# Falling column order in the dense products of a two-block network on one core

## The chip, the cores and the metric

The kernel runs on one core of a Trainium2 chip. The metric is the device time of one execution in microseconds (us). Three runs of the kernel before are at hand; one more execution was profiled.

## The reference

A sequence of 256 tokens with 1024 features goes through two small networks, one after the other. The parts that matter here are the dense products; everything between them (norms, rotary embedding, top-k attention, a recurrent scan, a convolution, a dilated attention) is left out:

```python
proj = h @ w_in                        # dsa: 1024 -> 2120 columns
y = o @ w_o                            # dsa_out: 1024 -> 1024
x = x + relu(h @ w_up) ** 2 @ w_down   # mlp0 and mlp1: 1024 -> 4096 -> 1024
r, k, v = mixed @ w_rkv                # rkv, then rwkv_out
... = h @ conv_w_in                    # conv: 1024 -> 4096, then conv_out
... = h @ dil_w_in                     # dil: 1024 -> 8192, then dil_out
```

All are float32. The kernel makes each product in three parts: a number is split into a rounded high part (`hi`, type fp32r) and the low rest (`lo`, fp32r), and hi x hi, hi x lo and lo x hi are added in PSUM.

## The kernel before

Weights come from HBM as granules of 128 x 1024 f32 into a ring of four slots (`raw`). ScalarE rounds a granule into `w_hi` (line 737), VectorE subtracts it to get `w_lo` (line 1350), and TensorE multiplies. Each of the three engines has one instruction order, written out by hand, and semaphores (`hi_ready`, `lo_ready`, `granule_used`) that count whole granules. So TensorE waits for a granule to be split, and the ring's slot comes free when its last matmul has ended.

Each matmul has a stationary operand (128 x 128, loaded by the weight load that goes with it), a moving operand (128 partitions x 256 or 512 columns) and an output tile of as many columns in one of the eight PSUM banks of 512 columns. The dense products come in two forms:

- by features (`feature_granule`, lines 2308 to 2310, and `entering_features`, line 2325): a 128-column piece of the weights is stationary, and the activation (`hi[:, kt, :]`, 256 tokens) moves. A granule holds two blocks of 128 input features by 512 output features and gives 24 matmuls of 256 columns.
- by tokens (`token_tile`, lines 2263 to 2265; `token_halves`, 2275 to 2277; `entering_tokens`, 2345; the value columns of the attention's input, 2536 to 2538; `down_tile` of the feed-forward, 2658 to 2660): 128 tokens of the activation are stationary, and 256 or 512 weight columns move.

The middle steps of the feed-forward and of the last projection are hardware loops (`pe.Fori`); the slots and banks in them are constants, and only the counts that are waited for depend on the loop's register.

The change leaves alone all other matmuls: plain f32 products (lines 2745, 2755, 2767), transposes (2375, 2401), the turns through a diagonal matrix (`turn_scaled`, line 2390), the broadcasts of the modulation (2724, 2730), the scan (2877 and others), the attention, the first granule of all (`opening_granule`) and the index columns. Two of these write PSUM columns in an order that isn't simply rising. In `turn_scaled` with `ordered=True` (the last turn, before the dilated attention's projection) the output is

```python
dst = bank[banks[b]][:, kk * SEQ:(kk + 1) * SEQ].rearrange("p (i f a l) -> p f a i l", i=TILES, f=TILES, a=32)[:, i]
```

with l of size 2 and i of stride 128: pairs of neighbouring columns, with a jump of 128 columns between them. `turn_heads` (line 2375) writes pairs with a stride of 4 columns.

Of the kernel before, what the change touches and what calls it, by code (L numbers as in the profile page):

```python
# [14 lines left out]
P = 128  # L15
# [11 lines left out]
BLOCK = 512  # L27
PER_BLOCK = 4
RING = 4
# [125 lines left out]
def program(nc, A, out):  # L155
    parts, parts_bf = shape_constants()
    with ExitStack() as keep:
# [29 lines left out]
        w_hi = sb("w_hi", [P, RING, GRAN], F32R)  # L187
        w_lo = sb("w_lo", [P, RING, GRAN], F32R)
# [16 lines left out]
        view, at = {}, 0  # L205
# [4 lines left out]
        at = 0  # L210
# [1134 lines left out]
        def _(dve):  # L1345
# [906 lines left out]
            conv()  # L2252
            dilated()

        @block.tensor
        def _(pe):
            def token_tile(i, slot, hi, lo, kts, n, dst, first, last):

                for kk, kt in enumerate(kts):
                    at = slice(kk * n, (kk + 1) * n)  # L2260
                    x_hi, x_lo = hi[:, kt, i * P:(i + 1) * P], lo[:, kt, i * P:(i + 1) * P]
                    begin, end = first and kk == 0, last and kk == len(kts) - 1
                    pe.matmul(dst, x_hi, w_hi[:, slot, at], start=begin, stop=False, skip_group_check=True)  # L2263
                    pe.matmul(dst, x_hi, w_lo[:, slot, at], start=False, stop=False, skip_group_check=True)  # L2264
                    mm = pe.matmul(dst, x_lo, w_hi[:, slot, at], start=False, stop=end, skip_group_check=True)  # L2265
                return mm

            def token_halves(i, slot, hi, lo, q, dst, parts=range(4)):

                for part in parts:  # L2270
                    kk, h = part // 2, part % 2
                    cols = slice(kk * BLOCK + h * SEQ, kk * BLOCK + (h + 1) * SEQ)
                    x_hi, x_lo = (x[:, 2 * q + kk, i * P:(i + 1) * P] for x in (hi, lo))
                    to = dst[:, h * SEQ:(h + 1) * SEQ]
                    pe.matmul(to, x_hi, w_hi[:, slot, cols], start=q == part == 0, stop=False, skip_group_check=True)  # L2275
                    pe.matmul(to, x_hi, w_lo[:, slot, cols], start=False, stop=False, skip_group_check=True)  # L2276
                    mm = pe.matmul(to, x_lo, w_hi[:, slot, cols], start=False, stop=q == PER_BLOCK - 1 and kk == 1, skip_group_check=True)  # L2277
                return mm

            def halves_granule(g, hi, lo, q, banks, begun=0):  # L2280
# [37 lines left out]
            def entering_features(g, slot, hi, lo, q, banks, rounded, split, change=False):  # L2318

                def term(w, x, begin, end):  # L2320
                    for f in range(4):
                        dst = banks[f // 2][:, (f % 2) * SEQ:(f % 2 + 1) * SEQ]
                        for kk in range(2):
                            at = slice(kk * BLOCK + f * P, kk * BLOCK + (f + 1) * P)
                            mm = pe.matmul(dst, w[:, slot, at], x[:, 2 * q + kk, :], start=begin and kk == 0 and f % 2 == 0,  # L2325
                                           stop=end and kk == 1, skip_group_check=True)
# [12 lines left out]
            def entering_tokens(gs, hi, lo, qs, banks, tiles, rounded, split):  # L2339

                def term(x, w, begin, end):
                    for i in tiles:
                        for g, q in zip(gs, qs):
                            for kk in range(2):
                                mm = pe.matmul(banks[i], x[:, 2 * q + kk, i * P:(i + 1) * P], w[:, g % RING, kk * BLOCK:(kk + 1) * BLOCK],  # L2345
                                               start=begin and q == kk == 0, stop=end and q == PER_BLOCK - 1 and kk == 1, skip_group_check=True)
# [99 lines left out]
            def dsa():  # L2446
                base = STREAM["dsa"]
                hi, lo = act_hi[0], act_lo[0]
# [75 lines left out]
                for q in range(PER_BLOCK):  # L2524
                    g = base + 4 + q
                    slot = g % RING
                    pe.wait_ge(lo_ready, g + 1)
                    feature_granule(g, slot, hi, lo, q, (bank[2],), range(2), False)
                    for i in range(TILES):
                        for kk in range(2):  # L2530
                            kt = 2 * q + kk
                            at = slice(kk * BLOCK + KV_COLS, (kk + 1) * BLOCK)
                            x_hi, x_lo = hi[:, kt, i * P:(i + 1) * P], lo[:, kt, i * P:(i + 1) * P]
                            dst = bank[3][:, i * KV_COLS:(i + 1) * KV_COLS]
                            begin, end = q == 0 and kk == 0 and i == 0, q == PER_BLOCK - 1 and kk == 1
                            pe.matmul(dst, x_hi, w_hi[:, slot, at], start=begin, stop=False, skip_group_check=True)
                            pe.matmul(dst, x_hi, w_lo[:, slot, at], start=False, stop=False, skip_group_check=True)
                            mm = pe.matmul(dst, x_lo, w_hi[:, slot, at], start=False, stop=end, skip_group_check=True)
# [101 lines left out]
            def mlp(l):  # L2640
                base, done = STREAM[f"mlp{l}"], 2 * FF_STEPS * l
                hi, lo = act_hi[0], act_lo[0]
# [8 lines left out]
                def down_tile(i, n, q, at_slot, slot, first, last):  # L2651

                    x_hi, x_lo = (m[:, slot, q, i * P:(i + 1) * P] for m in (M["hi"], M["lo"]))
                    wide = SEQ
                    for h in range(BLOCK // wide):
                        at = slice(n * BLOCK + h * wide, n * BLOCK + (h + 1) * wide)
                        dst = bank[2 + 2 * i + n][:, h * wide:(h + 1) * wide]
                        pe.matmul(dst, x_hi, w_hi[:, at_slot, at], start=first and q == 0 and h == 0, stop=False, skip_group_check=True)  # L2658
                        pe.matmul(dst, x_hi, w_lo[:, at_slot, at], start=False, stop=False, skip_group_check=True)  # L2659
                        mm = pe.matmul(dst, x_lo, w_hi[:, at_slot, at], start=False, stop=last and q == PER_BLOCK - 1, skip_group_check=True)  # L2660
                    return mm

                def wait_down(it, k0, q):
# [575 lines left out]
```

## Time and profile before

| | |
|---|---|
| median of 3 runs | 1062.45 us (1061.2 to 1068.3) |
| span of the profiled execution | 1066.7 us |
| TensorE matmuls busy | 1048.1 us (98%), 10480 matmuls |
| VectorE busy | 771.7 us (72%) |
| ScalarE busy | 590.3 us (55%) |
| GpSimd busy | 120.4 us (11%) |
| DMA | 192.23 MB, mean 180 GB/s |

The span is the time from the first to the last instruction of one profiled execution; no separate run time is given for that execution. Its span is 4.3 us above the median of the three runs and lies between the lowest and the highest of them. Matmuls are pipelined, and the duration of one reaches into the next, so busy time says that the engine has work and not how fast it goes; the pace comes from how many start in a stretch.

### The profile page before, as it was taken

Reading aid. Unit: us, or ns where it says so; the run is one execution under the profiler, and the core shown is the slowest. Engines: PE = TensorE matmul, PEld = TensorE weight load, DVE = VectorE, ACT = ScalarE, POOL = GpSimd, SP = SyncE. Lnnn points to the kernel's source line nnn. Section 1 sums busy time; section 2 is a strip of 40 time slices with the busy share of each in tenths; the row PEclk is TensorE's granted clock in tenths of the full one; section 3 lists DMA queues with packets and bytes.
Section 4 is the critical chain, followed back from the end, with each engine's and each line's share of the span. In section 5 each row is a group of like instructions: output and inputs, shape, how many; then the busy total and the mean of one; then the engine's idle time right before and its main releaser. Section 6 shows DMA issues by size and latency. Waiting matters only on the chain.

```text
span 1066.7 us, 25458 instructions
## 1 busy us (share of the span) xinstructions
PE 1048.1 (98%) x10480; PEld 996.2 (93%) x10485; DVE 771.7 (72%) x1090; ACT 590.3 (55%) x900; POOL 120.4 (11%) x131
## 2 busy tenths in 40 slices
PE   9999999999999999999999999999999999999997
PEld 8966999999999899997899999999998999999985
DVE  5987666766789689768766676786676877775586
ACT  6586555555456783334555454564544667666452
POOL 0230010100000028841000000000000000000000
PEclk9999999999999999999999999999999999999999
DMA  8734687888634510002678777737653656556401
GB/s 308 251 90 137 216 286 266 271 296 280 204 122 155 163 61 5 3 11 74 217 250 287 255 252 264 276 121 228 197 192 112 212 181 199 171 195 196 143 2 59
DMA packets 83073, 192.23 MB, mean 180 GB/s; under 512 B 6000, under 2 KB 6912, under 8 KB 82992
## 3 DMA queue, kind: packets, MB, share of 16 engines
q1 hardware_dynamic: 74256, 159.93, 45.3%
q0 software_dynamic: 7584, 27.53, 7.8%
q10 hardware_dynamic: 1152, 3.59, 1.0%
q8 instruction: 63, 1.03, 0.4%
q14 instruction: 18, 0.15, 0.0%
HBM read 189.45 MB, written 1.05 MB: 179 GB/s over the span
## 4 chain that ended last, share of the span: by engine, by line
PE 88%; DVE 6%; issue 2%; ACT 2%; DMA 2%; POOL 0%; DVEq 0%; POOLq 0%; ACTq 0%
PE bank L2308 13%; PE bank L2310 13%; PE bank L2309 13%; PE bank L2659 5%; PE bank L2658 5%; PE bank L2660 5%; PE bank L2325 4%; PE bank L2345 4%; PE bank L2877 4%; PE bank L2275 2%; PE bank L2276 2%; PE bank L2277 2%; PE bank L2263 1%; PE bank L2265 1%; PE bank L2264 1%
## 5 line engine op out<-in xcount | busy, mean ns | idle before, releaser
L1350 DVE TENSOR_TENSOR w_lo<-raw,w_hi 128x1024 fp32r<-128x1024 f32 x295 | 357.8, 1223 | 199.2 <-ACT w_hi L737 198.7
L737 ACT ACTIVATE w_hi<-raw 128x1024 fp32r<-128x1024 f32 x295 | 310.3, 1059 | 291.4 <-PE bank L2310 150.4
L2308 PE MATMUL bank<-act_hi,w_hi 128*128 128x256 f32 x1200 | 334.0, 278 | 0.4 <-DVE w_lo L1350 0.3
L2309 PE MATMUL bank<-act_lo,w_hi 128*128 128x256 f32 x1200 | 332.9, 277 | 0.0
L2310 PE MATMUL bank<-act_hi,w_lo 128*128 128x256 f32 x1200 | 332.8, 277 | 0.0
L2308 PEld LDWEIGHTS bank<-act_hi,w_hi 128*128 128x128 f32 x1200 | 225.3, 188 | 1.7 <-DVE w_lo L1350 0.9
L2310 PEld LDWEIGHTS bank<-act_hi,w_lo 128*128 128x128 f32 x1200 | 225.3, 188 | 0.0
L2309 PEld LDWEIGHTS bank<-act_lo,w_hi 128*128 128x128 f32 x1200 | 225.0, 187 | 0.0
L2658 PE MATMUL bank<-w_hi,ff_hi 128*128 128x256 f32 x512 | 141.5, 276 | 0.0
L2659 PE MATMUL bank<-w_lo,ff_hi 128*128 128x256 f32 x512 | 141.5, 276 | 0.0
L2660 PE MATMUL bank<-w_hi,ff_lo 128*128 128x256 f32 x512 | 141.5, 276 | 0.0
L2658 PEld LDWEIGHTS bank<-w_hi,ff_hi 128*128 128x128 f32 x512 | 96.1, 188 | 0.0
L2660 PEld LDWEIGHTS bank<-w_hi,ff_lo 128*128 128x128 f32 x512 | 96.1, 188 | 0.0
L2659 PEld LDWEIGHTS bank<-w_lo,ff_hi 128*128 128x128 f32 x512 | 96.1, 188 | 0.0
L590 POOL DMA_DIRECT2D mod_w<-in_w_mod_dram x48 | 25.8, 538 | 319.2 <-DVE mod_all L1666 239.2
L2275 PE MATMUL bank<-w_hi,act_hi 128*128 128x256 f32 x192 | 54.2, 282 | 0.0
L2276 PE MATMUL bank<-w_lo,act_hi 128*128 128x256 f32 x192 | 53.8, 280 | 0.0
L2277 PE MATMUL bank<-w_hi,act_lo 128*128 128x256 f32 x192 | 53.8, 280 | 0.0
L1666 DVE SCALAR_TENSOR_TENSOR mod_all<-mod_w,c_col,mod_all 128x1024 f32<-128x1024 f32 x42 | 52.5, 1278 | 0.0
L561 POOL TENSOR_TENSOR stat<-stat,half_neg 128x1 f32<-128x1 f32 x10 | 5.5, 553 | 405.9 <-DVE stat L1364 372.6
L2275 PEld LDWEIGHTS bank<-w_hi,act_hi 128*128 128x128 f32 x192 | 36.7, 191 | 1.0 <-issue 1.0
L2276 PEld LDWEIGHTS bank<-w_lo,act_hi 128*128 128x128 f32 x192 | 36.0, 188 | 0.0
(375 smaller groups left out, 1675.4 us busy)
## 6 DMA issues: line engine op xcount, KB each, us to landing
raw<-in_mlp_w_up_dram SPq DMA_DIRECT2D x64, 512.0 KB, 3.7
raw<-in_mlp_w_down_dram SPq DMA_DIRECT2D x64, 512.0 KB, 6.1
raw<-in_dil_w_in_dram SPq DMA_DIRECT2D x64, 512.0 KB, 4.1
mod_w<-in_w_mod_dram POOLq DMA_DIRECT2D x48, 512.0 KB, 5.9
raw<-in_conv_w_in_dram SPq DMA_DIRECT2D x32, 512.0 KB, 4.5
raw<-in_rwkv_w_rkv_dram SPq DMA_DIRECT2D x24, 512.0 KB, 4.1
raw<-in_dsa_w_in_dram SPq DMA_DIRECT2D x12, 512.0 KB, 8.1
raw<-in_dsa_w_o_dram SPq DMA_DIRECT2D x8, 512.0 KB, 4.5
```

The source lines that it names most:

```text
L737: act.activation(w_hi[:, slot, :], raw[:, slot, :], ACT.Copy).then_inc(hi_ready, 1)
L1350: dve.tensor_tensor(w_lo[:, slot, :], raw[:, slot, :], w_hi[:, slot, :].bitcast(F32), ALU.subtract).then_inc(lo_ready, 1)
L1666: dve.scalar_tensor_tensor(total, part, c, total, ALU.mult, ALU.add).then_inc(mod_used[n], 1)
L2275: pe.matmul(to, x_hi, w_hi[:, slot, cols], start=q == part == 0, stop=False, skip_group_check=True)
L2276: pe.matmul(to, x_hi, w_lo[:, slot, cols], start=False, stop=False, skip_group_check=True)
L2277: mm = pe.matmul(to, x_lo, w_hi[:, slot, cols], start=False, stop=q == PER_BLOCK - 1 and kk == 1, skip_group_check=True)
L2308: pe.matmul(dst, w_hi[:, slot, at], hi[:, kt, :], start=begin, stop=False, skip_group_check=True)
L2309: pe.matmul(dst, w_hi[:, slot, at], lo[:, kt, :], start=False, stop=False, skip_group_check=True)
L2310: mm = pe.matmul(dst, w_lo[:, slot, at], hi[:, kt, :], start=False, stop=end, skip_group_check=True)
L2658: pe.matmul(dst, x_hi, w_hi[:, at_slot, at], start=first and q == 0 and h == 0, stop=False, skip_group_check=True)
L2659: pe.matmul(dst, x_hi, w_lo[:, at_slot, at], start=False, stop=False, skip_group_check=True)
L2660: mm = pe.matmul(dst, x_lo, w_hi[:, at_slot, at], start=False, stop=last and q == PER_BLOCK - 1, skip_group_check=True)
```

## The change

A helper takes an operand, moves its start address to the last column and negates the step of the last dimension. It is put around the moving operand and the output of every dense product in the two forms above. The stationary operand, the order of matmuls, the waits and the flags stay.

```diff
+        def falling(x):
+            x = x[:, :]
+            steps = [list(pair) for pair in x.ap]
+            first = x.offset + steps[-1][0] * (steps[-1][1] - 1)
+            return bass.AP(x.tensor, first, steps[:-1] + [[-steps[-1][0], steps[-1][1]]])
...
-                        pe.matmul(dst, w_hi[:, slot, at], hi[:, kt, :], start=begin, stop=False, skip_group_check=True)
-                        pe.matmul(dst, w_hi[:, slot, at], lo[:, kt, :], start=False, stop=False, skip_group_check=True)
-                        mm = pe.matmul(dst, w_lo[:, slot, at], hi[:, kt, :], start=False, stop=end, skip_group_check=True)
+                        pe.matmul(falling(dst), w_hi[:, slot, at], falling(hi[:, kt, :]), start=begin, stop=False, skip_group_check=True)
+                        pe.matmul(falling(dst), w_hi[:, slot, at], falling(lo[:, kt, :]), start=False, stop=False, skip_group_check=True)
+                        mm = pe.matmul(falling(dst), w_lo[:, slot, at], falling(hi[:, kt, :]), start=False, stop=end, skip_group_check=True)
```

The same is done in `token_tile`, `token_halves`, `entering_features`, `entering_tokens`, the value columns and `down_tile`.

## Rows read from the trace of the kernel before

**Rows 1.** The page: span, busy time of three engines, TensorE's granted clock in 40 slices.

```profile
span 1066.7 us, 25458 instructions
...
PE 1048.1 (98%) x10480; PEld 996.2 (93%) x10485; DVE 771.7 (72%) x1090; ACT 590.3 (55%) x900; POOL 120.4 (11%) x131
...
PEclk9999999999999999999999999999999999999999
```

**Rows 2.** The page: the chain that ended last, by engine.

```profile
PE 88%; DVE 6%; issue 2%; ACT 2%; DMA 2%; POOL 0%; DVEq 0%; POOLq 0%; ACTq 0%
```

**Rows 3.** Groups of TensorE by shape: count, busy us, mean ns of one.

```profile
L2308 PE MATMUL bank<-act_hi,w_hi 128*128 128x256 f32 x1200 | 334.0, 278 | 0.4 <-DVE w_lo L1350 0.3
...
L2658 PE MATMUL bank<-w_hi,ff_hi 128*128 128x256 f32 x512 | 141.5, 276 | 0.0
...
L2275 PE MATMUL bank<-w_hi,act_hi 128*128 128x256 f32 x192 | 54.2, 282 | 0.0
...
L2263 PE MATMUL bank<-w_hi,act_hi 128*128 128x512 f32 x72 | 28.7, 399 | 0.0
...
L2325 PE MATMUL bank<-act_hi,w_hi 128*128 128x256 f32 x184 | 25.6, 281 | 0.6 <-ACT act_hi L768 0.6
...
L2345 PE MATMUL bank<-w_hi,act_hi 128*128 128x512 f32 x56 | 15.8, 404 | 0.1
...
L2536 PE MATMUL bank<-w_hi,act_hi 128*128 128x256 f32 x16 | 4.5, 279 | 0.0
```

**Rows 4.** Windows of TensorE alone: stretch, its length, busy us (matmuls), clock, DMA share, GB/s.

```profile
180.00:290.00 110.00, 110.00 (x970) 1.00 0.80 270
...
830.00:950.00 120.00, 120.00 (x1021) 1.00 0.60 193
```

**Rows 5.** Timeline of TensorE near 100 us: start, length, instruction, count (512 columns).

```profile
99.62 1.10 PE L2345 MATMUL bank<-w_lo,act_hi 128*128 128x512 f32 x4
100.55 1.10 PE L2345 MATMUL bank<-w_hi,act_lo 128*128 128x512 f32 x4
```

**Rows 6.** Timeline of TensorE near 352 us: plain f32 operands, 256 columns.

```profile
352.01 7.07 PE L2755 MATMUL bank<-act_f,g 128*80 128x256 f32 x32
359.01 1.07 PE L2813 MATMUL bank<-bk,const 128*32 128x256 f32 x16
```

**Rows 7.** Timeline of TensorE at three turns (ordered, plain, by heads) and their followers.

```profile
816.67 1.95 PE L2390 MATMUL bank<-per_head,X 128*128 128x128 f32 x16
818.45 1.88 PE L2730 MATMUL bank<-mod_all,const 128*128 128x512 f32 x4
820.29 2.05 PE L2390 MATMUL bank<-per_head,X 128*128 128x128 f32 x16
...
701.79 3.82 PE L2390 MATMUL bank<-per_head,xn 128*128 128x128 f32 x32
705.45 1.84 PE L2724 MATMUL bank<-const,mod_all 128*128 128x1 f32 x16
...
1038.66 0.60 PE L2375 MATMUL bank<-const,z_dil 128*128 128x128 f32 x4
1039.01 1.18 PE L2345 MATMUL bank<-w_hi,act_hi 128*128 128x512 f32 x4
```

**Rows 8.** TensorE's wait on a granule's low part, and VectorE's group that makes it.

```profile
PE bank L2308 <- DVE w_lo L1350: 0.3, 1, 0.3
...
L1350 DVE TENSOR_TENSOR w_lo<-raw,w_hi 128x1024 fp32r<-128x1024 f32 x295 | 357.8, 1223 | 199.2 <-ACT w_hi L737 198.7
```

More of the change, by code:

```diff
@@ L2262, in token_tile @@
                     begin, end = first and kk == 0, last and kk == len(kts) - 1
-                    pe.matmul(dst, x_hi, w_hi[:, slot, at], start=begin, stop=False, skip_group_check=True)
-                    pe.matmul(dst, x_hi, w_lo[:, slot, at], start=False, stop=False, skip_group_check=True)
-                    mm = pe.matmul(dst, x_lo, w_hi[:, slot, at], start=False, stop=end, skip_group_check=True)
+                    pe.matmul(falling(dst), x_hi, falling(w_hi[:, slot, at]), start=begin, stop=False, skip_group_check=True)
+                    pe.matmul(falling(dst), x_hi, falling(w_lo[:, slot, at]), start=False, stop=False, skip_group_check=True)
+                    mm = pe.matmul(falling(dst), x_lo, falling(w_hi[:, slot, at]), start=False, stop=end, skip_group_check=True)
                 return mm
@@ L2274, in token_halves @@
                     to = dst[:, h * SEQ:(h + 1) * SEQ]
-                    pe.matmul(to, x_hi, w_hi[:, slot, cols], start=q == part == 0, stop=False, skip_group_check=True)
-                    pe.matmul(to, x_hi, w_lo[:, slot, cols], start=False, stop=False, skip_group_check=True)
-                    mm = pe.matmul(to, x_lo, w_hi[:, slot, cols], start=False, stop=q == PER_BLOCK - 1 and kk == 1, skip_group_check=True)
+                    pe.matmul(falling(to), x_hi, falling(w_hi[:, slot, cols]), start=q == part == 0, stop=False, skip_group_check=True)
+                    pe.matmul(falling(to), x_hi, falling(w_lo[:, slot, cols]), start=False, stop=False, skip_group_check=True)
+                    mm = pe.matmul(falling(to), x_lo, falling(w_hi[:, slot, cols]), start=False, stop=q == PER_BLOCK - 1 and kk == 1, skip_group_check=True)
                 return mm
@@ L2324, in term @@
                             at = slice(kk * BLOCK + f * P, kk * BLOCK + (f + 1) * P)
-                            mm = pe.matmul(dst, w[:, slot, at], x[:, 2 * q + kk, :], start=begin and kk == 0 and f % 2 == 0,
+                            mm = pe.matmul(falling(dst), w[:, slot, at], falling(x[:, 2 * q + kk, :]), start=begin and kk == 0 and f % 2 == 0,
                                            stop=end and kk == 1, skip_group_check=True)
@@ L2344, in term @@
                             for kk in range(2):
-                                mm = pe.matmul(banks[i], x[:, 2 * q + kk, i * P:(i + 1) * P], w[:, g % RING, kk * BLOCK:(kk + 1) * BLOCK],
+                                mm = pe.matmul(falling(banks[i]), x[:, 2 * q + kk, i * P:(i + 1) * P], falling(w[:, g % RING, kk * BLOCK:(kk + 1) * BLOCK]),
                                                start=begin and q == kk == 0, stop=end and q == PER_BLOCK - 1 and kk == 1, skip_group_check=True)
@@ L2535, in dsa @@
                             begin, end = q == 0 and kk == 0 and i == 0, q == PER_BLOCK - 1 and kk == 1
-                            pe.matmul(dst, x_hi, w_hi[:, slot, at], start=begin, stop=False, skip_group_check=True)
-                            pe.matmul(dst, x_hi, w_lo[:, slot, at], start=False, stop=False, skip_group_check=True)
-                            mm = pe.matmul(dst, x_lo, w_hi[:, slot, at], start=False, stop=end, skip_group_check=True)
+                            pe.matmul(falling(dst), x_hi, falling(w_hi[:, slot, at]), start=begin, stop=False, skip_group_check=True)
+                            pe.matmul(falling(dst), x_hi, falling(w_lo[:, slot, at]), start=False, stop=False, skip_group_check=True)
+                            mm = pe.matmul(falling(dst), x_lo, falling(w_hi[:, slot, at]), start=False, stop=end, skip_group_check=True)
                     mm.then_inc(granule_used, 1)
@@ L2657, in down_tile @@
                         dst = bank[2 + 2 * i + n][:, h * wide:(h + 1) * wide]
-                        pe.matmul(dst, x_hi, w_hi[:, at_slot, at], start=first and q == 0 and h == 0, stop=False, skip_group_check=True)
-                        pe.matmul(dst, x_hi, w_lo[:, at_slot, at], start=False, stop=False, skip_group_check=True)
-                        mm = pe.matmul(dst, x_lo, w_hi[:, at_slot, at], start=False, stop=last and q == PER_BLOCK - 1, skip_group_check=True)
+                        pe.matmul(falling(dst), x_hi, falling(w_hi[:, at_slot, at]), start=first and q == 0 and h == 0, stop=False, skip_group_check=True)
+                        pe.matmul(falling(dst), x_hi, falling(w_lo[:, at_slot, at]), start=False, stop=False, skip_group_check=True)
+                        mm = pe.matmul(falling(dst), x_lo, falling(w_hi[:, at_slot, at]), start=False, stop=last and q == PER_BLOCK - 1, skip_group_check=True)
                     return mm
```

## The prediction

> **What bounds the kernel now.** I read the page's first two parts, then the chain that ended last, then the groups of TensorE by shape, then windows and stretches of its timeline, because the change touches nothing but the operands of matmuls. The reader is to see first that TensorE is busy 1048.1 of 1066.7 us and idle for 18.6, that VectorE and ScalarE have 295 and 476 us of free time, and that TensorE's granted clock is 9 tenths or more in all 40 slices, so this is one single stretch at the upper of its two levels, 2.4 GHz [rows 1]. The chain agrees: 88% of it is TensorE [rows 2]. Whatever the change does to the time from one matmul to the next therefore comes out in the end nearly in full. A few per cent of the matmuls' records can be missing, so I take paces only from stretches whose counts are plausible.
>
> The "mean ns of one" of a matmul is no pace. A matmul of 256 columns shows 276 to 282 ns [rows 3], yet 970 of them start in 110 us [rows 4]: they overlap, and the pace is 110 / 970 = 113.4 ns. That is the number that counts. Another dense stretch, 830 to 950 us, has 1021 in 120 us, or 117.5 ns [rows 4]. I take 115 ns for the whole kernel. With 512 columns four matmuls take 100.55 - 99.62 = 0.93 us, or 233 ns each [rows 5]. At 2.4 GHz one column takes 0.417 ns, so 256 columns are 106.7 ns and 512 are 213.3: the changed matmuls run within 6 to 10% of one column a tick, and no wait stands between them.
>
> **The change part by part.** Counted from the groups, the changed matmuls of 256 columns are 3 x 1200 + 3 x 512 + 3 x 192 + 3 x 184 + 3 x 16 = 6312, and those of 512 columns 3 x 72 + 3 x 56 = 384 [rows 3] (each line of rows 3 stands for three of the same count, one for each product of a high and a low part). They hold 6312 x 0.115 + 384 x 0.233 = 726 + 89 = 815 us of TensorE's time. The other 250 us (the scan, the attention, transposes, the last norm and the output) keep their operands as they are.
>
> Removed and added: no instruction, no wait, no semaphore increment, no DMA. The helper runs when the program is built and gives each matmul another start address and a step of -1 instead of 1. All the slots and banks are constants there, also inside the loops, so no register arithmetic is added to TensorE's queue; cost nothing, and there is no cover that could go. The order of matmuls, the weight loads, the flags and the columns that each writes stay. Both operands fall, so column c of the moving tile still goes to column c of PSUM, and two products that add to one tile still touch each column exactly one whole matmul apart. The readers of the banks wait for the whole group as before. Where VectorE fills w_lo (1223 ns a granule) it signals after the whole granule, so that no reader can start early or late because of the direction [rows 8].
>
> What is left is the price of a column that is read in falling order from SBUF and of one that is written in falling order to PSUM. No row of the trace shows a step of -1 on either side, so I bound it.
>
> From below: the column's own tick. If the 6.7 to 20 ns by which a matmul exceeds its columns were owed to the rising order, falling could give back at most 6312 x (115 - 106.7) + 384 x (233 - 213.3) = 52 + 8 = 60 us, which would be 1062 - 60 = 1002 us. Nothing in the trace ties that excess to the order, and I take none of it.
>
> From above: the nearest rows at half the column rate are the products whose operands are plain f32. There, 32 matmuls of 256 columns take 359.01 - 352.01 = 7.00 us, or 219 ns each [rows 6], and four of 512 columns take 820.29 - 818.45 = 1.84 us, or 460 ns each [rows 7]. If each column in falling order were taken by itself where two are taken together now, the changed matmuls would go at that pace: 6312 x (219 - 115) + 384 x (460 - 233) = 656 + 87 = 743 us more.
>
> Nearest to the change are the writes whose order isn't simply rising. The turn at 816.67 us (line 2390, ordered) writes 128 columns as pairs, each pair 128 columns from the one before, and 16 of them take 818.45 - 816.67 = 1.78 us, 111 ns each [rows 7]. The same operation with plain rising columns takes (705.45 - 701.79) / 32 = 114 ns [rows 7]. The transposes at 1038.66 us write pairs 4 columns apart, four in 0.35 us [rows 7]. So the PSUM side doesn't need a rising run of columns, and a jump after each pair is free. These rows keep the order inside a pair, and falling turns exactly that round. They also spend twice as long on a column as the changed products, so they could hide a loss that the change would show. I take zero because a falling pair still lies in the same two neighbouring words as the rising one, and the rows with jumps show that neighbourhood within a pair and not the direction of travel is what the writes are served by; both ends stay for the range.
>
> The Trainium skill speaks against this. Its page "PSUM — Partial Sum Buffer", section "Specifications (TRN2)", says that PSUM has lines of 8 bytes and that any non-contiguous access pattern slows matmuls significantly; "Advanced Engine Details and Errata", section "PSUM Cachelines", asks that every two consecutive elements be contiguous. By the first wording the turn at 816.67 us should be slow, and it isn't; by the second it may be fast, and a falling pair is an open case. For the moving tile, "SBUF Cachelines" on the same page asks for two accesses in a row to one line of 16 bytes; falling columns make four, as rising ones do, and by that rule the reads cost nothing more.
>
> **The rivals.** (a) *No change.* The address pattern is followed at the same pace in either direction: 1062 us. For it: the rows with jumps, and the lack of any added instruction. Against it: no row with a negative step. That the change does not do what it says (the pattern reaches the engine as a rising one) would give the same time, and is counted here, with 3 of the 54 in 100.
>
> (b) *Half rate.* The slower end, one mechanism: in a product at one column a tick, two neighbouring columns are served in one access, and the pair is only recognised when the second lies above the first. Its place is the PSUM write or the moving read of 6696 matmuls; its price is 743 us by the rows above. It decides from the first matmul on, since TensorE has no slack there. Of the 18.6 us of idle time [rows 1], a wait such as the 0.3 us of line 2308 for w_lo [rows 8] would vanish in it, as the weights would be ready long before; I take 15 us off. 1062 + 743 - 15 = 1790 us. If the pace were exactly two ticks a column (213.3 and 427 ns) the sum would be 6312 x 98.3 + 384 x 194 - 15 = 680 us and the time 1742. For it: the changed products are the ones that run close to one column a tick, the only ones that need pairs served together. Against it: nothing but the rows with jumps. It is also what the rule on PSUM's lines gives in this kernel, in the strict reading of the Trainium skill's page "PSUM — Partial Sum Buffer".
>
> (c) *A small price a matmul.* A falling tile starts on an odd column (255 or 511), and a lost tick or a short refill there costs a few ns a matmul. From 1.6 ns on (10.6 / 6696) it is over 1%. The pace of the same matmuls already differs by 117.5 - 113.4 = 4.1 ns between two stretches [rows 4]; by that much it would be 6696 x 4.1 = 27 us, 1090 us.
>
> (d) *Faster.* The excess of 6.7 to 20 ns shrinks, since reads of the moving tile and the weight load meet in another order: at most 1002 us, and half of it 1032.
>
> **How the numbers follow.** A measurement of this kernel can tell about 1%, 10.6 us, from no change; the three runs shown span 1061.2 to 1068.3. The profiled execution spans 1066.7 us, 4.3 above the median of 1062.45 and inside those three, so I add the sums to 1062. Chances: (a) 0.54, (b) 0.36, (c) 0.06, (d) 0.04. The likeliest is (a), 1062 us, and its own range is 1054 to 1072. Leaving (b) out would leave more than 2 in 10 out, so the range reaches over it: up to 1810, the 1790 with the spread of the paces. The low end is that of (a), since (d) has 4 in 100. Faster by over 1%: (d), 0.04. Slower by over 1%: (b) and most of (c), 0.41. Within 1%: the rest, 0.55.
>
> **What would show it.** In the changed kernel's windows the dense stretch from 180 to 290 us should again hold about 970 matmuls, the groups of line 2308 should stay near 278 ns, and four of 512 columns should take 0.93 us. Under (b) that stretch would hold about 500, with VectorE's and ScalarE's shares of the span falling by 40% and TensorE's staying at 98%. Under (c) all three would be off by a few ns. The unchanged stretches (the scan from 399 to 486 us, line 2390) should keep their lengths in every case; if they don't, the cause isn't the direction. My prediction is wrong above all if the order within a pair matters, which no row here tests.

## The result

The changed kernel takes 1092.88 us (median of 4 runs, 1092.71 to 1093.33) against 1061.83 us before: a ratio of 1.0267, with a 95% interval of 1.0224 to 1.0310. It is slower by 31 us, where no change was forecast.

The page of the changed kernel, its span, busy times and chain:

```profile
span 1091.2 us, 25458 instructions
...
PE 1073.8 (98%) x10480; PEld 1022.0 (94%) x10485; DVE 772.2 (71%) x1090; ACT 590.3 (54%) x900; POOL 119.9 (11%) x131
...
PEclk9999999999999999999999999999999999999999
...
PE 90%; DVE 5%; issue 1%; DMA 1%; ACT 1%; DVEq 0%; POOLq 0%; POOL 0%; ACTq 0%
...
L2314 PE MATMUL bank<-act_hi,w_hi 128*128 128x256 f32 x1200 | 339.1, 283 | 0.0
```

The instruction count and the granted clock are those of [rows 1]; VectorE and ScalarE are as busy in us as before. TensorE has 25.7 us more and the span 24.5. The mean of one matmul in the largest group went from 278 [rows 3] to 283 ns, which looks like nothing much; the pace is what to read. A window of TensorE in the changed kernel, the columns as in [rows 4]:

```profile
180.00:290.00 110.00, 110.00 (x927) 1.00 0.78 264
```

In that stretch 927 matmuls stand where 970 stood [rows 4]: 118.7 ns each, not 113.4. And its timeline for the kinds that were costed apart (512 columns; plain f32):

```profile
99.94 1.09 PE L2351 MATMUL bank<-w_hi,act_hi 128*128 128x512 f32 x4
100.87 1.10 PE L2351 MATMUL bank<-w_lo,act_hi 128*128 128x512 f32 x4
...
361.06 7.07 PE L2761 MATMUL bank<-act_f,g 128*80 128x256 f32 x32
368.06 1.07 PE L2819 MATMUL bank<-bk,const 128*32 128x256 f32 x16
```

Four falling matmuls of 512 columns take 0.93 us, as in [rows 5]. The plain f32 products keep their 7.00 us [rows 6], and the ordered turn takes 840.31 - 838.53 = 1.78 us in the changed kernel too [rows 7]. So the loss is all in the 6312 matmuls of 256 columns.

Their starts fall on a few levels. Before, a feature product starts 113.3 or 117.8 ns after the one ahead of it, for tens of us on end. It is 113.3 throughout the convolution and in both feed-forwards behind their first 20 us, and 117.8 in those 20 us, in the second block's first products and in the dilated attention's. After, the feature products are at 120.0 ns and the token products at 117.8. By stages, from the start of each one's first product, the first feed-forward lost 7.2 us, the second 7.3, the convolution 5.1, the dilated attention 2.6, the second block 1.0 and the first attention 0.8, with 0.4 before it: 24.4 of the 24.5.

The other 6.5 us of the 31 are in the kernel before. Its runs on one chip fall into two groups: of the 13 beside the first experiments, nine took 1060.5 to 1063.7 us and four 1067.5 to 1068.7. The profiled one, 1066.7 us, is of the second: its dilated attention ran at 117.8. A later kernel with the same paces elsewhere (halves, below) spans 1059.7 us and has that stretch at 113.3. The 1536 products of that stage at 4.4 ns each would be 6.8 of the 7.0 us between the two spans (an estimate). The changed kernel has no such spread (0.6 us).

### The profile page after: what moved, and what is told of

It is laid out like the page before. It is cut to its first block, busy times and chain, and to the rows that moved or that the text cites. A ratio compares the mean times of both kernels' runs of the same rounds, so it can differ in the third digit from the quotient of the medians.

```text
span 1091.2 us, 25458 instructions
## 1 busy us (share of the span) xinstructions
PE 1073.8 (98%) x10480; PEld 1022.0 (94%) x10485; DVE 772.2 (71%) x1090; ACT 590.3 (54%) x900; POOL 119.9 (11%) x131
## 4 chain that ended last, share of the span: by engine, by line
PE 90%; DVE 5%; issue 1%; DMA 1%; ACT 1%; DVEq 0%; POOLq 0%; POOL 0%; ACTq 0%
PE bank L2314 13%; PE bank L2316 13%; PE bank L2315 13%; PE bank L2666 6%; PE bank L2665 6%; PE bank L2664 6%; PE bank L2331 5%; PE bank L2351 4%; PE bank L2883 3%; PE bank L2281 2%; PE bank L2283 2%; PE bank L2282 2%; PE bank L2269 1%; PE bank L2271 1%; PE bank L2270 1%
## 5 line engine op out<-in xcount | busy, mean ns | idle before, releaser
L2314 PE MATMUL bank<-act_hi,w_hi 128*128 128x256 f32 x1200 | 339.1, 283 | 0.0
L2316 PE MATMUL bank<-act_hi,w_lo 128*128 128x256 f32 x1200 | 338.5, 282 | 0.0
L2315 PE MATMUL bank<-act_lo,w_hi 128*128 128x256 f32 x1200 | 338.5, 282 | 0.0
L2666 PE MATMUL bank<-w_hi,ff_lo 128*128 128x256 f32 x512 | 144.5, 282 | 0.0
L2665 PE MATMUL bank<-w_lo,ff_hi 128*128 128x256 f32 x512 | 144.4, 282 | 0.0
L2283 PEld LDWEIGHTS bank<-w_hi,act_lo 128*128 128x128 f32 x192 | 36.1, 188 | 0.0
```

Source lines behind the costliest of these rows:

```text
L2283: mm = pe.matmul(falling(to), x_lo, falling(w_hi[:, slot, cols]), start=False, stop=q == PER_BLOCK - 1 and kk == 1, skip_group_check=True)
L2314: pe.matmul(falling(dst), w_hi[:, slot, at], falling(hi[:, kt, :]), start=begin, stop=False, skip_group_check=True)
L2315: pe.matmul(falling(dst), w_hi[:, slot, at], falling(lo[:, kt, :]), start=False, stop=False, skip_group_check=True)
L2316: mm = pe.matmul(falling(dst), w_lo[:, slot, at], falling(hi[:, kt, :]), start=False, stop=end, skip_group_check=True)
L2665: pe.matmul(falling(dst), x_hi, falling(w_lo[:, at_slot, at]), start=False, stop=False, skip_group_check=True)
L2666: mm = pe.matmul(falling(dst), x_lo, falling(w_hi[:, at_slot, at]), start=False, stop=last and q == PER_BLOCK - 1, skip_group_check=True)
```

## The experiments

All whole-network times are compared with runs of the kernel before on the same chip. "Feature form" and "token form" are those of the section on the kernel, here "feature products" and "token products". The letters and numbers of the theories are explained in the expectation where each first appears.

**Which side.** The two sides of a matmul apart; the tiles come out reversed, so what follows computes with reversed tiles.

```diff
-pe.matmul(falling(dst), w_hi[:, slot, at], falling(hi[:, kt, :]), ...)
+pe.matmul(falling(dst), w_hi[:, slot, at], hi[:, kt, :], ...)     # e1, in all dense products
+pe.matmul(dst, w_hi[:, slot, at], falling(hi[:, kt, :]), ...)     # e2, in all dense products
```

> Only the PSUM side of every dense product falls; the moving tile is read rising, so each output tile comes out with its columns in reverse order and what follows computes with reversed tiles. Theory W (a falling write costs a few ns a matmul): all of the loss stays, about 1093 us, with the feature products near 120 ns apart. Theory R (a falling read costs it): about 1062 us, paces of 113.4 and 117.7 ns as before. Theory P (the pace depends on how the moving reads stand to the weight loads, and falling reads never get into the fast one): as R.

> Only the moving tile is read in falling order; PSUM is written rising, so the tiles again come out reversed. Theory W: about 1062 us. Theories R and P: about 1093 us, feature products near 120 ns and token products near 117.8 ns. If both sides had a price of their own, this and the run before would each lose a part, together 31 us.

Measured: writes alone 1063.21 us (ratio 1.0002, 0.9972 to 1.0032); reads alone 1092.84 us (1.0274, 1.0229 to 1.0318). The same stretch in each, first with falling writes:

```profile
180.00:290.00 110.00, 110.00 (x970) 1.00 0.80 269
```

and with falling reads:

```profile
180.00:290.00 110.00, 110.00 (x927) 1.00 0.78 262
```

970 is the kernel before and 927 the changed one, to the matmul. Falling writes cost nothing that these runs can tell; the whole loss is the moving read. Theory W has fallen.

**Which form.** Both sides fall in one form only.

```diff
-outF, inF, outT, inT = falling, falling, falling, falling
+outF, inF, outT, inT = falling, falling, rising, rising     # e3: feature form alone
+outF, inF, outT, inT = rising, rising, falling, falling     # e4: token form alone
```

> Both sides fall in the feature form alone (4152 matmuls of 256 columns); the token form rises as before. From the paces of the changed kernel (feature products 115.6 to 120.2 ns, that is 4.6 ns each on 4152) all theories give about 19 us if the two forms are independent: 1081 us. If token products are fast only because the matmuls before them left the engine in its fast pace, they lose their 4.2 ns too and the time is 1088 to 1093 us.

> Both sides fall in the token form alone (2160 matmuls of 256 columns, 384 of 512). Independent forms: 1536 products of the feed-forward lose 4.2 ns each, about 7 us, 1069 us. If the fast pace of 113.4 ns is entered only by rising token products (in the kernel before it begins at the first product of line 2658, at 140.5 us, and holds through the feature products that follow), the feature products lose it as well: 2 x 768 in the feed-forward, some 500 in the first attention, at 4.3 ns each, 9 us more: about 1078 us.

Measured: 1091.46 us (1.0260) and 1078.67 us (1.0140, 1.0095 to 1.0184). Each alone they lose 29 and 16 us, and both at once 31, not 45: they are not independent. Each form slows the other. In e3 the token products rise, and in the feed-forwards they go at 117.8 ns, where they had 113.3 before. In e4 no feature product is touched, and yet the convolution's (740 to 790 us) go at 117.8 ns: 427 in 50 us, where the kernel before has 444:

```profile
740.00:790.00 50.00, 50.00 (x427) 1.00 0.62 190
880.00:940.00 60.00, 60.00 (x532) 1.00 0.63 202
```

The second row is the other way round: the dilated attention (880 to 940 us) is at 113.3 here, with 532 matmuls, and was at 117.8 with 512 in the profiled run of the kernel before. So rising feature products have two paces, and what else ran in the kernel changes which of them a stage gets. That can't be a price of a matmul's own falling order. The expectation's 1078 us was met, but not its mechanism, by which the fast pace is entered only through rising token products: the dilated attention has the fast pace here although the token products of all dense stages fall. (One product of `change_form`, which the change leaves alone, still rises, at 313 us; the feature products are at 117.8 ns on both sides of it.)

**What of the order.** Three other orders, on both sides of all dense products; each leaves the result as it is.

```diff
-return bass.AP(x.tensor, first, steps[:-1] + [[-steps[-1][0], steps[-1][1]]])
+return bass.AP(x.tensor, x.offset + 1, steps[:-1] + [[2, n // 2], [-1, 2]])            # e5: 1, 0, 3, 2, ...
+return bass.AP(x.tensor, x.offset + n - 2, steps[:-1] + [[-2, n // 2], [1, 2]])        # e6: 254, 255, 252, 253, ...
+return bass.AP(x.tensor, x.offset + n // 2, steps[:-1] + [[-(n // 2), 2], [1, n // 2]]) # e7: 128 to 255, 0 to 127
```

> Both sides of all dense products go up, but inside each pair the upper column comes first (1, 0, 3, 2, ...). If the order within a pair is what costs, 1093 us; if the direction of travel or the place where the read starts costs, 1060 to 1066 us.

> Both sides go down by pairs, and inside a pair rise (254, 255, 252, 253, ...). If the direction of travel costs, about 1093 us; if only the order within a pair does, 1060 to 1066 us.

> Each tile is read and written upper half first, rising within each half (128 to 255, then 0 to 127; for 512 columns 256 to 511 first). If only the start or the end of a moving read against the next weight load counts, and not its direction, the pace changes here as well (towards 1093 us or otherwise away from 1062); if each column's step counts, 1060 to 1066 us.

Measured: swapped pairs 1063.11 us (1.0018, 0.9984 to 1.0052), falling pairs 1092.71 us (1.0275, 1.0217 to 1.0333), halves 1061.91 us (1.0001, 0.9976 to 1.0026). Falling by pairs costs what falling by columns costs, to 0.2 us, though it starts on an even column and rises inside each pair. Swapped pairs start on an odd column and cost nothing. What costs is the direction of travel through the tile, not the order in a pair, the start column or the jump at a half. The halves kernel runs as fast as the faster group of the kernel before, and its trace shows how these runs probably look (none of them was profiled):

```profile
740.00:790.00 50.00, 50.00 (x443) 1.00 0.62 192
880.00:940.00 60.00, 60.00 (x532) 1.00 0.59 188
```

Both stretches are at 113.3, and its span is 1059.7 us.

**The products by themselves.** A kernel of nothing but matmuls, in parts of 96 on a line each; features with `w` stationary and `act` moving, tokens the other way. VectorE, ScalarE and the queues are idle and there is no wait.

```python
features(lambda d, s, m: pe.matmul(d, s, m, **K))                                    # line 119, 121, ...
features(lambda d, s, m: pe.matmul(order(d, "fall"), s, order(m, "fall"), **K))      # line 120
```

> Not the network: 26 parts of 96 matmuls (the 512-column ones 48), one after another on the same SBUF data, each on a line of its own, with no other engine at work and no waits between them. The output holds a few PSUM banks and nothing of the reference. Theory 1 (the pace comes from the engine's own two read streams): the levels 113.4, 117.8 and 120.0 ns of the network's kernels appear here too, with all other engines idle: falling features 120.0, falling reads with rising writes 120.0, falling writes with rising reads 113.4 or 117.8, falling token products 117.8. Theory 2 (it is contention with VectorE's and ScalarE's traffic in SBUF): all parts run at one pace, below 113.4 ns. For the other orders: if the order inside a pair of columns counts, the swapped pairs are slow and falling pairs and fours are fast; if the direction of travel counts, the reverse. 512 columns: no difference above 1 ns. Plain f32 operands and bf16 operands: within 1 ns by order if the loss belongs to the pairing with a weight load of fp32r.

Its timeline: start, length, line, operands, count. The pace of a part is the way to the next part's start over its count.

```profile
62.66 11.68 PE L119 MATMUL bank<-act,w 128*128 128x256 f32 x96
74.17 11.53 PE L120 MATMUL bank<-act,w 128*128 128x256 f32 x96
85.54 11.67 PE L121 MATMUL bank<-act,w 128*128 128x256 f32 x96
...
131.44 11.68 PE L125 MATMUL bank<-act,w 128*128 128x256 f32 x96
142.96 11.53 PE L126 MATMUL bank<-act,w 128*128 128x256 f32 x96
154.33 11.67 PE L127 MATMUL bank<-w,act 128*128 128x256 f32 x96
...
246.14 11.07 PE L135 MATMUL bank<-w,act 128*128 128x512 f32 x48
257.05 11.37 PE L136 MATMUL bank<-w,act 128*128 128x512 f32 x48
268.25 41.60 PE L137 MATMUL bank<-af,wf 128*128 128x256 f32 x192
```

Rising (119) takes 11.51 us, 119.9 ns each, and falling (120) 11.37 us, 118.4: here falling is the *faster* one. Falling writes alone (125) 120.0, falling reads alone (126) 118.4: again the read. Swapped pairs and halves (128, 134) gave 120.0, falling pairs and fours 118.4. Theory 2 is out, since the parts run at two paces with all other engines idle, and neither is below 113.4 ns. But the sign is the opposite of the network's, which none of my theories gave. With 512 columns the sign is the network's own: rising (135) 227.3 ns, falling (136) 233.3. Plain f32 (137, 192 records for 96 matmuls) takes 41.4 us both ways, and bf16 (139, 140) 109.2 ns between neighbouring starts, both ways. Beside the idle engines, two things differed from the network: the moving tiles start at the weights' place in a block of 512 bytes, and nothing adds up in PSUM.

**Places in SBUF.** The same parts with the moving tile shifted by `d` columns:

```python
flat[:, kt * 256 + d:kt * 256 + d + 256]     # d = 0 to 144; 144 columns (576 bytes) is the network's
```

> Not the network: parts of 96 matmuls each on a line of its own (512 columns: 48), no other engine at work, four bf16 matmuls between most parts; the output is nothing of the reference. In the part-by-part run before, the moving tiles began 0 bytes from the weights' place in a block of 512 bytes; in the network they begin 64 bytes beyond it (576 of 1024). Here the start of the moving tile is shifted by 0 to 64 columns (0 to 256 bytes) and by 144 columns (576 bytes, as in the network), rising and falling. Theory A (two read streams of TensorE, moving tile and weight load, get in each other's way by their places in SBUF): the pace depends on the shift; at 144 columns rising gives 113.4 or 117.8 ns and falling 120.0, at 0 rising 120.0 and falling 118.4 as before. Theory B (it is the adding up in PSUM): the parts with 144 columns that only write stay at 120.0 and 118.4, those that add go to 113.4 or 117.8 and 120.0. Theory C (the other engines' traffic, or the network's waits, set the pace): all parts at 120.0 and 118.4 ns. For the form of the product: a feature part straight after a rising token part runs at 113.4 and after a falling token part at 117.8 if the fast pace is entered through token products alone.

The parts at 144 columns (149 and 151 write, 153 and 155 add up; then tokens and the features behind them, rising in 161, falling in 164):

```profile
205.73 11.76 PE L151 MATMUL bank<-act,w 128*128 128x256 f32 x96
217.34 0.61 PE L115 MATMUL bank<-ab,wb 128*128 128x256 bf16 x4
217.70 11.55 PE L153 MATMUL bank<-act,w 128*128 128x256 f32 x96
229.09 0.61 PE L115 MATMUL bank<-ab,wb 128*128 128x256 bf16 x4
...
243.17 11.14 PE L161 MATMUL bank<-w,act 128*128 128x256 f32 x96
254.15 11.04 PE L162 MATMUL bank<-act,w 128*128 128x256 f32 x96
265.03 0.61 PE L115 MATMUL bank<-ab,wb 128*128 128x256 bf16 x4
265.40 11.55 PE L164 MATMUL bank<-w,act 128*128 128x256 f32 x96
276.79 11.47 PE L165 MATMUL bank<-act,w 128*128 128x256 f32 x96
288.10 0.61 PE L115 MATMUL bank<-ab,wb 128*128 128x256 bf16 x4
```

At the network's place falling features take 11.61 us (120.9 with the start behind bf16) and rising ones 11.39 (118.6): the network's sign. Writing and adding give the same, so theory B is out. Features straight behind rising tokens take 10.88 us, 113.3 ns, and behind falling tokens 11.31, 117.8: the network's levels, to 0.1 ns. With no shift they were 120.0 and 118.4. With 512 columns at the network's place (lines 167 and 169) 48 matmuls take 11.29 us in either direction, so the 6 ns of the first bench are gone as well. Theory A stands in this bench. The next run asks what leads into the fast pace.

> Not the network: groups of 48 feature products (shift of 144 columns, as in the network), a few token products, 48 feature products again; four bf16 matmuls ahead of each group; other engines idle, the output is nothing of the reference. Theory M (two steady paces for rising order, 117.8 and 113.4 ns; a rising token product or a few switch to the fast one, which then holds; falling order leaves it and never enters it): the first feature part of each group runs at 117.8, the one behind n rising token products at 113.4 from some n between 1 and 4 on, behind falling token products at 117.8; a falling feature part behind 12 rising token products runs at 120.0, and the rising feature part behind that at 117.8 again; four bf16 matmuls end the fast pace. Theory N (the pace is set by which operands are read, and what came before does not count): every rising feature part has the same pace.

Groups of feature products, a few rising token products, features again. Here with one token product (125), with six (141), and a falling feature part (158) that came behind twelve, with a rising one (159) after it:

```profile
33.27 0.28 PE L125 MATMUL bank<-w,act 128*128 128x256 f32 x1
33.39 5.82 PE L126 MATMUL bank<-act,w 128*128 128x256 f32 x48
39.05 0.61 PE L119 MATMUL bank<-ab,wb 128*128 128x256 bf16 x4
...
81.07 0.86 PE L141 MATMUL bank<-w,act 128*128 128x256 f32 x6
81.76 5.60 PE L142 MATMUL bank<-act,w 128*128 128x256 f32 x48
87.20 0.61 PE L119 MATMUL bank<-ab,wb 128*128 128x256 bf16 x4
...
131.40 5.92 PE L158 MATMUL bank<-act,w 128*128 128x256 f32 x48
137.16 5.81 PE L159 MATMUL bank<-act,w 128*128 128x256 f32 x48
142.81 0.61 PE L119 MATMUL bank<-ab,wb 128*128 128x256 bf16 x4
```

Behind one or two token products the features stay at 117.9 ns; behind three, four, six or twelve they are at 113.3 to 113.5. Falling features are at 120.0 behind twelve token products, and the rising ones behind those at 117.7. That is theory M, with one flaw: three groups came out of the bf16 matmuls in the fast pace already (115.0 to 115.2 ns with the start), and in the one of them that had twelve rising token products and then rising features, these were at 117.7. One rising token product of 512 columns behind the third such group did the same (117.9). A token run can switch in either direction.

**Switching in the network.** Three rising token products ahead of four feature stages, in the kernel before and in the changed one. The stretch that the expectation calls the convolution's (830 to 950 us) is in truth the dilated attention's.

```diff
+            def into_pace(b, x, g):
+                pe.wait_ge(lo_ready, g + 1)
+                for k in range(3):
+                    pe.matmul(bank[b][:, 0:SEQ], x[:, k % 2, 0:P], w_hi[:, g % RING, 0:SEQ], start=True, stop=True)
```

> The kernel before, rising order, with three token products of 256 columns put ahead of four feature stages (two of the values, keys and rates of the second block, the second of the convolution's input, the second of the dilated attention's); each writes a bank half that the next product overwrites. Theory M (rising order has two steady paces, and three token products switch from the slow one to the fast one): some 288 + 672 + 1056 products go from 117.8 to 113.4 ns, 9 us, less 12 x 0.12 = 1.4 us for the added ones: 1053 to 1055 us, with the convolution's stretch (830 to 950 us) at 113.4. If a switch only toggles, and the waits in the network spoil it, the time lies between 1055 and 1068 us. Theory N (no such switch in the network): 1063 us.

> The same twelve added products (rising themselves) in the changed kernel, all dense products falling. Theory M: falling feature products have one pace, 120.0 ns, that nothing switches: 1092.9 + 1.4 = 1094 us. Theory N or any theory in which falling order only fails to find the way into the fast pace: 9 to 13 us faster than the changed kernel, about 1082 us.

Measured: 1073.19 us (1.0099, 1.0084 to 1.0115) and 1093.44 us (1.0299, 1.0285 to 1.0313). The first is a miss: not 9 us faster but 11 slower. Its windows say why:

```profile
740.00:790.00 50.00, 50.00 (x427) 1.00 0.62 190
880.00:940.00 60.00, 60.00 (x512) 1.00 0.56 178
```

The convolution was in the fast pace (444 matmuls in the kernel before) and is out of it (427); so is the dilated attention, which the halves kernel has at 113.3. The timeline just ahead of the added products (L2322) tells the two apart, first the convolution, then the dilated attention:

```profile
718.25 1.07 PE L2331 MATMUL bank<-act_hi,w_lo 128*128 128x256 f32 x8
719.16 0.52 PE L2322 MATMUL bank<-w_hi,act_hi 128*128 128x256 f32 x3
...
837.76 1.10 PE L2331 MATMUL bank<-act_hi,w_lo 128*128 128x256 f32 x8
838.70 0.52 PE L2322 MATMUL bank<-w_hi,act_hi 128*128 128x256 f32 x3
```

In the convolution the eight products ahead of the added three take 0.91 us, 114 ns each: there three token products led out of the fast pace. In the dilated attention they take 0.94 us, 118 ns each: it was slow from its first products on, and stayed slow. The two places in the second block were at 117.8 ns ahead of the added products and behind them. So at none of the four places did three token products lead into the fast pace, as they did in the bench, and why the dilated attention began slow in this kernel isn't shown. The sizes fit: added matmuls 1.4 us, 672 products of the convolution at 4.4 ns each 3.0, and the 1536 of the dilated attention 6.8, against a run that has it fast, make 11.2 of the 11.3 us.

The falling kernel gained nothing either (0.6 us slower than 1092.88). Theory M expected that, but it tells little, since the added products gained nothing in the rising kernel.

**The decisive pair.** One tensor of 64 bytes a partition is allocated ahead of the weights' ring, not behind it; weights and activations then start at the same place in a block of 512 bytes, as in the first bench.

```diff
+        gain = sb("gain", [P, 2, KT])
         raw = sb("raw", [P, RING, GRAN])
...
-        gain = sb("gain", [P, 2, KT])
```

> Not the network: for each of 14 places of the moving tile (shifted by 0 to 124 columns of 4 bytes against the weights' place in a block of 512 bytes) 12 token products, 48 feature products, 3 token products, 48 feature products, all rising, then 48 feature products falling; other engines idle, the output is nothing of the reference. Theory A (places and direction together set the pace): rising parts at 120.0 for 0 columns, at 113.4 or 117.8 for 16 (the network's place), falling at 118.4 for 0 and 120.0 for 16; other places have paces of their own, and one may keep both rising parts at 113.4 or below. Theory D (falling order is slow as such): falling is above rising at every place.

> The kernel before with one small tensor (64 bytes a partition) allocated ahead of the weights' ring and not behind it, so that the weights and the activation tiles start at the same place in a block of 512 bytes, not 64 bytes apart. Nothing else changes. Theory A: rising products of 256 columns go at 120.0 ns as in the first part-by-part run, 6312 x about 5 ns = 31 us more, less 384 x 6 ns for the wide ones: about 1090 us. Theory D: 1062 us.

> The changed kernel with the same move. Theory A: falling products at 118.4 ns: about 6312 x 1.2 = 8 us less than the changed kernel's 1092.9, so 1085 us, and below the moved rising kernel. Theory D: 1093 us, 31 us above the moved rising kernel.

Measured: rising 1094.95 us (1.0296, 1.0266 to 1.0327), falling 1086.95 us (1.0221, 1.0191 to 1.0251). With the weights moved by 64 bytes, falling order is the faster by 8.0 us, where before it was the slower by 31; the ranges of their runs (1094.26 to 1095.56, 1086.63 to 1087.19) lie far apart. Both are slower than the kernel before, and 5 and 2 us above what was expected. The rising kernel, moved:

```profile
180.00:290.00 110.00, 110.00 (x919) 1.00 0.78 258
```

and the falling one, moved:

```profile
180.00:290.00 110.00, 110.00 (x932) 1.00 0.78 261
```

919 against 932: 119.7 against 118.0 ns. With 512 columns the moved kernels go the other way: about 227 ns rising and 233 falling, as in the first bench. In the bench of places, at no shift and at 16 columns (the network's 64 bytes), features rising (125, 127; 149, 151) and falling (128; 152):

```profile
35.19 5.92 PE L127 MATMUL bank<-act,w 128*128 128x256 f32 x48
40.95 5.84 PE L128 MATMUL bank<-act,w 128*128 128x256 f32 x48
46.64 0.61 PE L119 MATMUL bank<-ab,wb 128*128 128x256 bf16 x4
...
106.23 5.61 PE L149 MATMUL bank<-act,w 128*128 128x256 f32 x48
111.67 0.52 PE L150 MATMUL bank<-w,act 128*128 128x256 f32 x3
112.03 5.82 PE L151 MATMUL bank<-act,w 128*128 128x256 f32 x48
117.69 5.91 PE L152 MATMUL bank<-act,w 128*128 128x256 f32 x48
123.44 0.61 PE L119 MATMUL bank<-ab,wb 128*128 128x256 bf16 x4
```

Rising 120.0 and falling 118.5 at none; rising 113.3 or 117.9 and falling 119.8 at 16. Of the 14 places, 16, 48, 80 and 112 columns have 113.3 to 113.5 for one of the two rising parts and 117.7 to 117.9 for the other; no place kept both fast, so the bench pointed to no faster kernel. Other places have other paces, such as 116.7 ns at 4 columns. Theory D has fallen.

## Why the prediction was wrong

The step that failed is the part that begins "Nearest to the change": that a column read in falling order costs what a rising one does, so that (a), no change, is likeliest. It weighed the PSUM write at length and settled the moving read in one sentence, so that the read's term in the sum was nothing. For the write that was right: it costs nothing (e1, 1063.21 us). The read costs all of the 31 us (e2, 1092.84 us).

The rows I used for it couldn't have settled it. The writes with jumps [rows 7] say something of PSUM, and no row had another read order. What the trace did have is [rows 4]: the same matmuls at 113.4 ns in one stretch and 117.5 in another. I took their mean, 115 ns, as *the* pace, and used the difference only to price rival (c). Two paces for the same instruction with no wait in between were the sign that the pace depends on something outside the instruction.

Rival (c), given 6 in 100, came out at the measured time: 4.1 ns each, 1090 us, against 1093. That its price came so near is luck in the main: it borrowed the distance between two paces without saying what they are, and the larger part of the loss happens to be the fast pace that is gone (4.4 of the 6.7 ns that a fast feature product lost). Its mechanism was wrong. It laid the price on the odd start column; a start on an odd column costs nothing (e5, 1063.11 us), and a start on an even one with the same direction costs all (e6, 1092.71 us).

Rival (b), half rate at 1790 us with 36 in 100, didn't happen on either side, and it alone stretched the range to 1810. The bound by rows of plain f32 was misread as well: line 2755 has 16 matmuls in the code and 32 records in the trace, so a plain f32 matmul is two records, and 219 ns is the pace of a record. The mechanism given for half rate, a pair that is recognised only when it rises, is out by the swapped pairs (e5). So is the prediction's own sign of being wrong, that the order within a pair matters. The excess over one column a tick, of which the prediction said that nothing in the trace ties it to the order, is just where the change acts: from 6.7 or 11.1 ns to 13.3 in the feature form. Rival (d), given 4 in 100, named the meeting of the moving reads and the weight load, which is near the conflict that fits the runs (it is argued, see below), but with the opposite sign. In the moved kernels falling order does give some of the excess back, 8 us.

No added work, the unchanged kinds at their old pace, and the loss coming out in the end almost in full (25.7 us of busy time, 24.5 of span): all as written. With 512 columns the forecast of no change held in the network, by luck of its place: in the first bench and in the moved kernels falling costs 6 ns there.

The rules that were weighed come next. The Trainium skill's page "PSUM — Partial Sum Buffer", section "Specifications (TRN2)", says that any non-contiguous pattern slows matmuls significantly. Falling writes and swapped pairs are such patterns here and cost nothing (ratios of 1.0002 and 1.0018). By the Trainium skill's page "Advanced Engine Details and Errata", section "SBUF Cachelines", falling reads would go at full pace, since they hit each line as often as rising ones; the measured 31 us decide against it as the only rule for reads. A third I had not weighed: the Trainium skill's page "TensorE: Matmul & The Clock Gate", section "Step-by-step: what each phase is for", says that loading the next weights takes no SBUF read bandwidth from the running matmul. Moving the weights, and the tensors between them and `gain`, by 64 bytes against the activations took the rising kernel from 1062.73 to 1094.95 us, and shifting the moving tile alone did the like in the bench: their relation counts. Whether bandwidth is what is lost no run here shows.

What stays open: why the levels are 113.3, 117.8, 118.4 and 120.0 ns; what exactly throws a stretch into one or the other; and whether it is the weight load's reads that the moving reads meet. That the direction and the relative place set the pace is shown in the bench and in the network. That what ran before counts too is shown, but no rule for it holds in both. A conflict in SBUF between the two read streams fits all of it, and is argued, not shown. A reversed weight load, which would test it, wasn't tried.

## What to carry to other kernels

Where TensorE runs without gaps, plot the time between the starts of like matmuls along the kernel before costing anything. If it sits on two levels, as 113.3 and 117.8 ns here, up to 4% of these products' time hangs on placement and order, and any change that touches an operand's address, direction or the sequence of forms can win or lose it without adding an instruction. A result such as "falling is slower" then belongs to one layout: 64 bytes turned it round here, and with 512 columns it came out differently again. When such a change is tried, try it at a second offset too.

## What the runs showed of the hardware

- At the two relative places that the networks used, back-to-back fp32r matmuls of 256 columns with a weight load each took 113.3, 117.8, 118.4 or 120.0 ns, with other engines busy or idle alike, by the moving tile's direction and its place in 512 bytes against the weights', and by what ran before. Other places in the bench had other paces (116.7 ns at 4 columns). A stage of rising products at the network's place holds 113.3 or 117.8 ns from end to end, and two profiled spans of 1066.7 and 1059.7 us differ by the pace of one stage.
- With 512 columns the pace was 227 ns rising and 233 falling where weights and moving tiles start at the same place in 512 bytes, and 233 both ways at the network's place.
- Products of the two forms act on each other: three rising token products took rising features from 117.9 to 113.3 ns in the bench, and in the network three of them led the convolution out of the fast pace; twelve added ones (1.4 us of work) cost 11 us in all.
- Falling PSUM writes beside rising reads kept the rising pace (e1, and line 125 of the first bench). Swapped pairs and halves, written and read alike, kept it too.
- bf16 products of 256 columns ran at 109.2 ns rising and falling; 96 plain f32 ones left 192 records, 215.8 ns each, both ways.
